# Small buffers placed between the stationary operands of a float32r matmul kernel

## The chip, the cores and the metric

The kernel runs on one core of a Trainium2 chip. The metric is the device time of one execution in microseconds (us). TensorE has two clock levels, 1.2 and 2.4 GHz; the granted clock in the profile is given as a share of the upper one.

## The reference, cut to what matters

Two layers work on an activation of 256 rows by 1024 columns in float32. Each layer is a SwiGLU feed-forward block, a mixer of three attention branches, and a second feed-forward block; a last norm ends it.

```python
for l in range(DEPTH):                                   # 2
    x = x + 0.5 * _swiglu(_rmsnorm(x, ffn1_norm[l]), ffn1_w_gate[l], ffn1_w_up[l], ffn1_w_down[l])
    h = _rmsnorm(x, mix_norm[l])
    ... = jnp.split(h @ w_in[l], cuts, axis=-1)
    y_a = _dsa_attention(...) @ w_branch_a[l]
    y_b = _moba_attention(...) @ w_branch_b[l]
    y_c = _nsa_attention(...) @ w_branch_c[l]
    g = jax.nn.sigmoid(m_g.reshape(B, T, N_BRANCH, D))
    x = x + (g[:, :, 0] * y_a + g[:, :, 1] * y_b + g[:, :, 2] * y_c) @ w_out[l]
    x = x + 0.5 * _swiglu(_rmsnorm(x, ffn2_norm[l]), ffn2_w_gate[l], ffn2_w_up[l], ffn2_w_down[l])
return _rmsnorm(x, final_norm)
```

## The kernel before

Every large product is done with a float32r trick: both operands are split into a high and a low part, and three matmuls replace one (`three`, lines 1371 to 1373): high activation by high weight, high activation by low weight, low activation by high weight. The same three kinds stand in `by_pieces` (line 1421), which serves the first two slabs and the one after them at the start of the kernel.

The weights of the model are the moving operand: a slab of 2048 float32 per partition is loaded by DMA into `raw`, ScalarE writes the high part `whi` (line 1114) and VectorE the low part `wlo` (line 536). Each of the three has three slots of 8192 bytes per partition. A matmul streams 512 columns of a slab (2048 bytes per partition), in the last projection slabs (`M_LAST`) 220 columns, so that there column block kk of a slab begins at kk times 880 bytes.

The activations are the stationary operand, 128 columns of float32 (512 bytes per partition) for each matmul: `ht_hi` and `ht_lo` (the turned, normed x, 8 blocks of 256 columns), `at_hi` and `at_lo` (the gated product of a feed-forward step, or the heads of a branch), and `bt_hi` and `bt_lo` (the same for the step before the last one and for other heads). Each of these 128 columns is loaded into TensorE by an LDWEIGHTS of its own, since no two matmuls in a row have the same stationary operand.

The tensors in SBUF (`sb(...)`) lie one behind another in each partition in the order in which they are declared. Ahead of `ht_hi` stand `raw`, `whi`, `wlo` and `x`, with 24576, 24576, 24576 and 8192 bytes; `ht_hi` and `ht_lo` have 8192 bytes each, `at_*` and `bt_*` 2048 each. All of these are multiples of 512, so every slab's start, every 512-column block and every stationary operand has the same place modulo 512.

The small tensors of the change belong to the attention stage. `cgt` holds the gates of branch C (written at line 1292 by ScalarE, lines 898 and 900 by VectorE), `top8` the eight largest scores of a selection round, `nmax` the negated row maxima (line 751) that the exponentials on ScalarE (line 1247) take as bias, and `den` the row sums, read by the reciprocal at line 785.

The queues: SyncE issues the weight DMAs three slabs ahead; ScalarE and VectorE convert the slabs and do the work of the stage between the conversions; TensorE goes through the slabs in order, with transposes (lines 1390, 1546, 1613, 1672) and the small float32 matmuls of the attention (1585, 1632, 1641) between them. The order is written out by hand and the waits are on semaphores. The change touches neither.

Of the kernel before, what the change touches and what calls it, by code (L numbers as in the profile page):

```python
# [33 lines left out]
P = 128  # L34
SEQ, D, DFF, DEPTH = 256, 1024, 2816, 2
NT = SEQ // P
# [96 lines left out]
def build(nc, x_in, ffn1_w_gate, ffn1_w_up, ffn1_w_down, w_in, cmp_w1_k, cmp_w2_k, cmp_w1_v, cmp_w2_v,  # L133
# [3 lines left out]
    with ctx:  # L137
        def sb(name, shape, dt=F32):
            return ctx.enter_context(nc.sbuf_tensor(name, shape, dt))
# [6 lines left out]
        whi = sb("whi", [P, 3, SLAB], F32R)  # L146
        wlo = sb("wlo", [P, 3, SLAB], F32R)
        x = sb("x", [P, NT, D])
        ht_hi = sb("ht_hi", [P, KD, SEQ], F32R)
        ht_lo = sb("ht_lo", [P, KD, SEQ], F32R)  # L150
        at_hi = sb("at_hi", [P, 2, SEQ], F32R)
        at_lo = sb("at_lo", [P, 2, SEQ], F32R)
        bt_hi = sb("bt_hi", [P, 2, SEQ], F32R)
        bt_lo = sb("bt_lo", [P, 2, SEQ], F32R)
        scr = sb("scr", [P, 4 * SEQ])
# [47 lines left out]
        rstd = sb("rstd", [P, NT])  # L203
        hrstd = sb("hrstd", [P, NT])
        work = sb("work", [P, 384])
        top8 = sb("top8", [P, NT, 8])

        sel_b = sb("sel_b", [P, 384])
        future_b = sb("future_b", [P, 384])
        nmax = sb("nmax", [P, 2, 16])  # L210
        den = sb("den", [P, 2, 16])
        rden = sb("rden", [P, 2, 16])
        cgt = sb("cgt", [P, NT, 24])
        cgt3 = cgt[:, :, :].rearrange("p t (h b) -> p t h b", b=3)
        hid = sb("hid", [P, 64])
        hid2 = sb("hid2", [P, 64])
# [1699 lines left out]
```

## Time and profile before

| | us |
|---|---|
| median of 2 runs | 1163.97 (1163.6 to 1164.35) |
| the profiled execution | 1163.91 |
| its span, first to last instruction | 1162.2 |
| TensorE busy | 1153.9 |
| VectorE busy | 951.5 |
| ScalarE busy | 581.7 |
| GpSimd busy | 31.9 |

The profile is one execution. PE is TensorE's matmuls, PEld its weight loads, which run beside the matmuls. A matmul's record reaches from its start to the end of its drain, so the records of a dense stretch overlap: the distance from one start to the next is what a matmul costs there, not the length of its record. The chain of work that ended last takes that into account. "x4" is a count, "128x512" are partitions by elements.

### The profile page before, as it was taken

How to read it: one execution, taken by the hardware profiler on the slowest of the kernel's cores; microseconds unless marked ns; L12 is line 12 of the kernel's file. 1: busy time of each engine (PE TensorE's matmuls, PEld its weight loads, DVE VectorE, ACT ScalarE, POOL GpSimd, SP SyncE). 2: the span in 40 equal slices, each digit the busy share in tenths (PEclk: the TensorE clock that was granted, in tenths of full speed). 3: DMA queues.
4: the chain of work that ended last, by engine and by line, in shares of the span. 5: the costliest groups of instructions: out<-in, count | busy, mean ns of one | idle time of the engine just before them, and what ended most of it. 6: DMA issues, size and time to landing. Idle time of an engine off the chain costs nothing.

```text
span 1162.2 us, 16328 instructions
## 1 busy us (share of the span) xinstructions
PE 1153.9 (99%) x5573; PEld 945.9 (81%) x5573; DVE 951.5 (82%) x1788; ACT 581.7 (50%) x757; POOL 31.9 (3%) x67
## 2 busy tenths in 40 slices
PE   9999999999999999999999999999999999999997
PEld 7888888887778888888888888888877788888886
DVE  6877788899977687778887887878999696888777
ACT  6444345447764464344454444454578635434433
POOL 2000000001000000000000000000010000000000
PEclk9999999999999999999999999999999999999999
DMA  8566554765425555655556556556653335655561
GB/s 285 190 214 216 181 188 163 234 203 163 137 80 182 181 157 204 217 191 185 195 177 202 180 173 215 182 189 191 198 180 110 141 135 184 219 181 169 202 234 38
DMA packets 148996, 211.04 MB, mean 182 GB/s; under 512 B 8160, under 2 KB 109136, under 8 KB 148944
## 3 DMA queue, kind: packets, MB, share of 16 engines
q1 hardware_dynamic: 148256, 209.64, 54.5%
q10 hardware_dynamic: 688, 0.71, 0.2%
q8 instruction: 31, 0.51, 0.2%
q14 instruction: 21, 0.17, 0.0%
HBM read 209.28 MB, written 1.05 MB: 181 GB/s over the span
## 4 chain that ended last, share of the span: by engine, by line
PE 99%; DVE 0%; issue 0%; ACT 0%; POOLq 0%; POOL 0%; DVEq 0%
PE ps L1371 30%; PE ps L1373 30%; PE ps L1372 30%; PE ps L1585 2%; PE ps L1421 1%; PE ps L1641 1%; PE ps L1613 1%; PE ps L1390 1%; PE ps L1546 1%; PE ps L1558 0%; PE ps L1765 0%; PE ps L1672 0%; PE ps L1632 0%; DVE x L1000 0%; PE ps L1573 0%
## 5 line engine op out<-in xcount | busy, mean ns | idle before, releaser
L1114 ACT ACTIVATE whi<-raw 128x2048 fp32r<-128x2048 f32 (+1 forms) x195 | 365.9, 1879 | 253.3 <-PE ps L1373 252.2
L536 DVE TENSOR_TENSOR wlo<-raw,whi 128x2048 fp32r<-128x2048 f32 (+1 forms) x195 | 433.9, 2244 | 65.6 <-ACT whi L1114 45.7
L1371 PE MATMUL ps<-whi,ht_hi 128*128 128x512 f32 (+1 forms) x1192 | 465.6, 391 | 0.2
L1373 PE MATMUL ps<-whi,ht_lo 128*128 128x512 f32 (+1 forms) x1192 | 460.8, 387 | 0.0
L1372 PE MATMUL ps<-wlo,ht_hi 128*128 128x512 f32 (+1 forms) x1192 | 460.3, 386 | 0.0
L1373 PEld LDWEIGHTS ps<-whi,ht_lo 128*128 128x128 f32 x1192 | 223.9, 188 | 45.9
L1371 PEld LDWEIGHTS ps<-whi,ht_hi 128*128 128x128 f32 x1192 | 224.0, 188 | 45.0 <-issue 1.4
L1372 PEld LDWEIGHTS ps<-wlo,ht_hi 128*128 128x128 f32 x1192 | 224.1, 188 | 43.9
L598 DVE STREAM_TRANSPOSE scr<-scr 32x128 f32<-32x128 f32 x688 | 208.3, 303 | 10.3
L1371 PE MATMUL ps<-whi,at_hi 128*128 128x512 f32 x304 | 118.5, 390 | 0.0
L1372 PE MATMUL ps<-wlo,at_hi 128*128 128x512 f32 x304 | 118.3, 389 | 0.0
L1373 PE MATMUL ps<-whi,at_lo 128*128 128x512 f32 x304 | 118.3, 389 | 0.0
L1154 ACT ACTIVATE scr<-ps,rstd 128x256 f32<-128x256 f32 x88 | 36.9, 471 | 130.7 <-PE ps L1373 130.2
L588 DVE SCALAR_TENSOR_TENSOR scr<-ps,rstd,scr 128x256 f32<-128x256 f32 x88 | 38.5, 479 | 56.0 <-ACT scr L1154 56.0
L1371 PEld LDWEIGHTS ps<-whi,at_hi 128*128 128x128 f32 x304 | 57.1, 188 | 12.5 <-issue 0.8
L1373 PEld LDWEIGHTS ps<-whi,at_lo 128*128 128x128 f32 x304 | 57.1, 188 | 11.9
L1372 PEld LDWEIGHTS ps<-wlo,at_hi 128*128 128x128 f32 x304 | 57.1, 188 | 11.9
L1247 ACT ACTIVATE prob<-prob,nmax 128x128 f32<-128x128 f32 (+1 forms) x96 | 42.4, 446 | 6.7 <-DVE nmax L751 6.7
L1142 ACT ACTIVATE ht_hi<-ps,cols 128x256 fp32r<-128x256 f32 x47 | 19.2, 472 | 30.4 <-PE ps L1390 30.4
L1213 ACT ACTIVATE proj<-ps,rstd 128x512 f32<-128x512 f32 (+1 forms) x24 | 14.2, 645 | 35.6 <-PE ps L1373 35.6
L1260 ACT ACTIVATE p_t<-ps 128x512 f32<-128x512 f32 x36 | 20.1, 592 | 19.6 <-PE ps L1613 14.3
L560 DVE SCALAR_TENSOR_TENSOR ht_lo<-ps,cols,ht_hi 128x256 fp32r<-128x256 f32 x48 | 20.6, 477 | 10.9 <-ACT ht_hi L1142 10.8
(176 smaller groups left out, 757.3 us busy)
## 6 DMA issues: line engine op xcount, KB each, us to landing
raw<-in_ffn_w_down_dram SPq DMA_DIRECT2D x88, 512.0 KB, 4.9
raw<-in_w_in_dram SPq DMA_DIRECT2D x88, 512.0 KB, 4.5
raw<-in_ffn_w_gate_dram SPq DMA_DIRECT2D x85, 512.0 KB, 4.0
raw<-in_ffn_w_up_dram SPq DMA_DIRECT2D x85, 512.0 KB, 5.0
raw<-in_w_out_dram SPq DMA_DIRECT2D x16, 512.0 KB, 4.4
raw<-in_w_branch_c_dram SPq DMA_DIRECT2D x8, 512.0 KB, 4.4
raw<-in_w_branch_b_dram SPq DMA_DIRECT2D x4, 512.0 KB, 3.9
raw<-in_w_branch_a_dram SPq DMA_DIRECT2D x4, 512.0 KB, 4.0
```

Source lines behind the costliest of these rows:

```text
L536: nc.vector.tensor_tensor(wlo[:, n, 0:w], raw[:, n, 0:w], whi[:, n, 0:w].bitcast(F32), ALU.subtract).then_inc(lo_done, 1)
L560: nc.vector.scalar_tensor_tensor(ht_lo[:, k, :], src, gain(l, n, k), ht_hi[:, k, :].bitcast(F32), ALU.mult, ALU.subtract).then_inc(htl, 1)
L588: nc.vector.scalar_tensor_tensor(act[:, t, :], ps[:, bank, FSTEP:2 * FSTEP], rstd[:, t:t + 1], sg[:, t, :], ALU.mult, ALU.mult).then_inc(a ...
L598: ins = nc.vector.transpose(dst[q:q + 32, :, :, a:a + 32], src[a:a + 32, :, :, q:q + 32])
L1114: nc.scalar.activation(whi[:, n, 0:w], raw[:, n, 0:w], ACT.Copy).then_inc(hi_done, 1)
L1154: nc.scalar.activation(sg[:, t, :], ps[:, t + step_bank(f, i), 0:FSTEP], ACT.Silu, scale=rstd[:, t:t + 1]).then_inc(silu_done, 1)
L1247: ins = nc.scalar.activation(pv, pv, ACT.Exp, scale=-1.0, bias=nmax[:, b, 4 * t + h:4 * t + h + 1], accum_out=den[:, b, 4 * t + h:4 * t + ...
L1260: nc.scalar.activation(p_t[:, f, :], ps[:, pt_bank(e, f), :], ACT.Copy).then_inc(pt_a, 1)
L1371: nc.tensor.matmul(o, xh, wh, start=start, stop=False)
L1372: nc.tensor.matmul(o, xh, wl, start=False, stop=False)
L1373: return nc.tensor.matmul(o, xl, wh, start=False, stop=stop)
L1585: ins = nc.tensor.matmul(score_head(t, h), q_t[row, qb + h // 2, t * P:(t + 1) * P], k_t[row, kb + kstep * (h // 2), 0:nk], start=opens, s ...
```

## The change

Four small tensors move in the list of declarations: `cgt` (192 bytes per partition) goes between `x` and `ht_hi`; `top8` (64) and `nmax` (128) go between `ht_lo` and `at_hi`; `den` (128) goes between `at_lo` and `bt_hi`. Against the moving operands, modulo 512, `ht_hi` and `ht_lo` then begin 192 bytes on, `at_hi` and `at_lo` 384 bytes on, and `bt_hi` and `bt_lo` at the same place again, as does everything from `scr` on up to where `top8` stood. The tensors declared behind that place move down by up to 512 bytes. No instruction is added, removed or moved.

```diff
@@ -146,10 +146,14 @@
         whi = sb("whi", [P, 3, SLAB], F32R)
         wlo = sb("wlo", [P, 3, SLAB], F32R)
         x = sb("x", [P, NT, D])
+        cgt = sb("cgt", [P, NT, 24])
         ht_hi = sb("ht_hi", [P, KD, SEQ], F32R)
         ht_lo = sb("ht_lo", [P, KD, SEQ], F32R)
+        top8 = sb("top8", [P, NT, 8])
+        nmax = sb("nmax", [P, 2, 16])
         at_hi = sb("at_hi", [P, 2, SEQ], F32R)
         at_lo = sb("at_lo", [P, 2, SEQ], F32R)
+        den = sb("den", [P, 2, 16])
         bt_hi = sb("bt_hi", [P, 2, SEQ], F32R)
         bt_lo = sb("bt_lo", [P, 2, SEQ], F32R)
         scr = sb("scr", [P, 4 * SEQ])
@@ -203,14 +207,10 @@
         rstd = sb("rstd", [P, NT])
         hrstd = sb("hrstd", [P, NT])
         work = sb("work", [P, 384])
-        top8 = sb("top8", [P, NT, 8])
 
         sel_b = sb("sel_b", [P, 384])
         future_b = sb("future_b", [P, 384])
-        nmax = sb("nmax", [P, 2, 16])
-        den = sb("den", [P, 2, 16])
         rden = sb("rden", [P, 2, 16])
-        cgt = sb("cgt", [P, NT, 24])
         cgt3 = cgt[:, :, :].rearrange("p t (h b) -> p t h b", b=3)
```

## Rows read from the trace of the kernel before

**Rows 1.** The page's chain that ended last: shares of the span, then lines.
```profile
PE 99%; DVE 0%; issue 0%; ACT 0%; POOLq 0%; POOL 0%; DVEq 0%
PE ps L1371 30%; PE ps L1373 30%; PE ps L1372 30%; PE ps L1585 2%; PE ps L1421 1%; PE ps L1641 1%; PE ps L1613 1%; PE ps L1390 1%; PE ps L1546 1%; PE ps L1558 0%; PE ps L1765 0%; PE ps L1672 0%; PE ps L1632 0%; DVE x L1000 0%; PE ps L1573 0%
```
**Rows 2.** Windows by stage: us, busy (xinstructions) per engine, granted clock, DMA share, GB/s.
```profile
600.00:700.00 100.00, 100.00 (x443) 82.81 (x442) 82.88 (x139) 44.42 (x38) 0.00 (x0) 1.00 0.56 188
...
800.00:900.00 100.00, 99.90 (x636) 81.53 (x635) 92.23 (x251) 65.26 (x137) 7.08 (x8) 1.00 0.54 166
```
**Rows 3.** Groups by form, PE, whole span: xcount | busy us, mean ns | idle us.
```profile
L1371 PE MATMUL ps<-whi,ht_hi 128*128 128x512 f32 x1160 | 456.8, 394 | 0.2
L1373 PE MATMUL ps<-whi,ht_lo 128*128 128x512 f32 x1160 | 452.0, 390 | 0.0
L1371 PE MATMUL ps<-whi,at_hi 128*128 128x512 f32 x304 | 118.5, 390 | 0.0
L1371 PE MATMUL ps<-whi,bt_hi 128*128 128x512 f32 x48 | 18.8, 393 | 0.0
L1371 PE MATMUL ps<-whi,ht_hi 128*128 128x220 f32 x32 | 8.8, 275 | 0.0
L1421 PE MATMUL ps<-whi,ht_hi 128*128 128x512 f32 x24 | 8.4, 432 | 0.0
L1632 PE MATMUL ps<-w_k,scr 128*128 128x256 f32 x16 | 4.1, 378 | 0.0
```
**Rows 4.** Timeline of PE, dense stretch: start us, us, instruction.
```profile
624.62 0.39 PE L1371 MATMUL ps<-whi,at_hi 128*128 128x512 f32 x1
...
625.98 0.39 PE L1371 MATMUL ps<-whi,at_hi 128*128 128x512 f32 x1
```
**Rows 5.** The chain in order of time: start us, us, line.
```profile
303.83 0.87 PE ps L1613 x8
...
307.44 0.86 PE ps L1632 x4
```
**Rows 6.** Timeline of PEld around a matmul with no weight load beside it.
```profile
336.81 0.19 PEld L1373 LDWEIGHTS ps<-whi,ht_lo 128*128 128x128 f32 x1
337.35 0.14 PEld L1641 LDWEIGHTS ps<-p_t,proj 128*64 128x64 f32 x2 [0.35 <-issue]
```
**Rows 7.** Groups by form, PE, 337.2 to 337.3 us: that one matmul.
```profile
L1373 PE MATMUL ps<-whi,ht_lo 128*128 128x512 f32 x1 | 0.4, 388 | 0.0
```
**Rows 8.** Groups by form, PE, 336.9 to 337.0 us: its neighbours before.
```profile
L1371 PE MATMUL ps<-whi,ht_hi 128*128 128x512 f32 x1 | 0.4, 389 | 0.0
L1372 PE MATMUL ps<-wlo,ht_hi 128*128 128x512 f32 x1 | 0.4, 389 | 0.0
```
**Rows 9.** Groups by form, PE, 244.86 to 244.90 us: the first narrow matmul.
```profile
L1371 PE MATMUL ps<-whi,ht_hi 128*128 128x220 f32 x1 | 0.3, 262 | 0.0
```
**Rows 10.** Timeline of PE, narrow matmuls: first one counted, and nine starts later.
```profile
245.06 0.27 PE L1373 MATMUL ps<-whi,ht_lo 128*128 128x220 f32 x1
...
246.07 0.27 PE L1373 MATMUL ps<-whi,ht_lo 128*128 128x220 f32 x1
```
**Rows 11.** Groups by form, PEld, 244.93 to 250.2 us: all narrow slabs.
```profile
L1373 PEld LDWEIGHTS ps<-whi,ht_lo 128*128 128x128 f32 x16 | 3.1, 192 | 0.0
L1372 PEld LDWEIGHTS ps<-wlo,ht_hi 128*128 128x128 f32 x16 | 3.1, 192 | 0.0
L1371 PEld LDWEIGHTS ps<-whi,ht_hi 128*128 128x128 f32 x15 | 2.9, 192 | 0.0
```
**Rows 12.** The page's groups, PEld: weight loads beside 512-column streams mostly.
```profile
L1373 PEld LDWEIGHTS ps<-whi,ht_lo 128*128 128x128 f32 x1192 | 223.9, 188 | 45.9
L1373 PEld LDWEIGHTS ps<-whi,at_lo 128*128 128x128 f32 x304 | 57.1, 188 | 11.9
```
**Rows 13.** Who waited for whom: us, times, longest us.
```profile
ACT whi L1114 <- PE ps L1373: 252.2, 93, 3.6
PEld ps L1613 <- DVE prob L804: 0.8, 2, 0.4
```
**Rows 14.** Instructions on nmax, den and cgt: ns min/median/max, us, forms.
```profile
L751 DVE DVE_READ_ACCUMULATOR2_ANT nmax<- x96: 81/83/85, 284.8 to 916.9; 128x1 f32 x96
L785 DVE RECIPROCAL rden<-den x24: 170/177/179, 289.1 to 919.4; 128x4 f32<-128x4 f32 x24
L804 DVE TENSOR_SCALAR prob<-prob,rden,cgt x32: 395/408/749, 299.5 to 904.0; 128x256 f32<-128x256 f32 x32
```

## The prediction

> **What bounds the kernel now.** I read the chain of work that ended last first: TensorE is 99% of it, and the three lines of the three-matmul product alone are 90% [rows 1]. The windows by stage say the same of each part: in a feed-forward stretch TensorE is busy for 100.00 of 100 us, VectorE for 82.88 and ScalarE for 44.42; in the attention stage TensorE 99.90, VectorE 92.23 [rows 2]. The granted clock is 1.00, the upper of the two levels, 2.4 GHz. The list of waits shows ScalarE waiting 252.2 us for TensorE to free a slab, and TensorE's own weight loads waiting 0.8 us for VectorE's scaled probabilities [rows 13]. So the time is a count of matmuls times the distance between two starts, and nothing that VectorE or ScalarE does a little faster or slower is seen.
>
> The count: 1160 + 304 + 48 + 24 groups of three 512-column float32r matmuls, 4608 in all [rows 3]. The distance: seven starts from 624.62 to 625.98 us, six steps, 1.36 / 6 = 0.2267 us [rows 4]. The product is 1044.6 us, 90% of the span, which agrees with the chain. Only this distance can move the time: 1% of it is 10 us.
>
> 512 columns at 2.4 GHz are 213.3 ns, so 13.3 ns of each step are something else. The profile has a yardstick: four plain float32 matmuls of 256 columns, each with its own 128-column weight load, follow each other in 0.86 / 4 = 215 ns [rows 5], and their records last 378 ns where the float32r ones last 389 [rows 3, 8]. So 226.7 - 215 = 11.7 ns are peculiar to the float32r stream. The change can be worth something only if these 11.7 ns, or a part, depend on where the stationary operand lies, or if a new cost appears.
>
> **The change part by part.** *Instructions.* None is added, removed or moved; no wait, no DMA and no queue changes. The moving operands and x don't move. What moves is the address of the stationary operands: 3 x (1160 + 304 + 24) = 4464 wide matmuls now have it 192 bytes (ht) or 384 bytes (at) on; 144 (bt) keep their place modulo 512 and are a control [rows 3].
>
> *The small tensors.* They are used in two short stages: 96 reads of the row maximum at 83 ns, 24 reciprocals at 177 ns, 32 scalings at 408 ns, besides a few more [rows 14]. I take 0. Were each VectorE instruction of these rows 10% slower, that is 0.1 x (96 x 0.083 + 24 x 0.177 + 32 x 0.408) = 2.5 us of VectorE work in all; the cover is VectorE's idle 7.8 us in each 100 of that stage and the slabs converted ahead [rows 2]; without the cover 2.5 us is the price.
>
> *The writes.* ScalarE and VectorE write ht, at and bt at the new addresses. Both have tens of us to spare in each 100 us of a feed-forward stage [rows 2]: 0.
>
> *The weight load itself.* It runs beside the preceding matmul. At its own pace it allows one matmul each 0.87 / 8 = 109 ns (eight 128-column transposes, each with a load of 128 columns) [rows 5]. Beside a wide matmul it has 226.7 ns. A slower load is therefore hidden until it costs 118 ns more, twice its length: 0 for 4464 loads. Only the 96 narrow matmuls of 220 columns are paced by it: were each load 4 ns slower, 0.4 us.
>
> *The stream beside the load.* This is the one term that counts. Both are reads of the same partitions. Today both begin at the same place modulo 512; the stream covers 2048 bytes in 226.7 ns (9.0 bytes per ns) and the load 512 bytes in at most 109 ns (4.7). The stream draws ahead at 4.3 bytes per ns and would come upon the load's place modulo 512 again only after 512 / 4.3 = 119 ns, when the load is over. With the operand 192 bytes on the stream passes it after 45 ns, with 384 after 89 ns, both within the load. If two reads at one place modulo 512 hinder each other, the before is the case with a meeting at the start only, and the after has one in the middle. Does the trace show any hindrance?
>
> First, today's: at 337.03 us a float32r matmul runs with no load beside it; the load before it starts at 336.81, and the next at 337.35 after 0.35 us of idle time [rows 6]. Its record is 388 ns [rows 7]; its neighbours with loads beside them have 389 each [rows 8]. So the load takes 1 ns from the stream and the 11.7 ns are there without it. Against the mean of the whole group of line 1373, 390 ns [rows 3], it is 2 ns. The ends of these records are modelled, which is why I don't call this proof. A second sign is that the excess goes with the columns: the first narrow matmul, not yet held by its weights, has 262 ns [rows 9]; (388 - 262) / 292 columns = 0.432 ns per column where 2.4 GHz gives 0.417. That is a slower stream, not a fixed loss to a load.
>
> Second, another place modulo 512: in the narrow slabs the column blocks begin at 0, 880 and 1760 bytes, that is 0, 368 and 224 modulo 512, so the stationary operand is 0, 144 and 288 bytes on. The 47 loads there all average 192 ns in their three groups [rows 11]; a dependence on place would have to show in them unless it were the same for all three. Beside wide matmuls the load has 188 [rows 12]. The distance is (246.07 - 245.06) / 9 = 112.2 ns [rows 10], against the 109 of the transposes. What this doesn't exclude: these streams have 275 ns against 262, so 13 ns of their record is waiting for weights [rows 3, 9], and a loss of the stream below that would be hidden.
>
> So the value I take for the term is 0 per matmul, the nearest rows in kind being 388 and 389. Below: the meeting of today is worth up to 2 ns, 4464 x 2 = 8.9 us gained. Above: a new meeting costs as much as a narrow stream and a load lose to each other, 112.2 - 108.7 = 3.5 ns, 15.6 us. The farthest bound is that stream and load are served in turn, 109 ns each, 487 us; nothing leans to it.
>
> The Trainium skill, page "TensorE: Matmul & The Clock Gate", section "Part 2: What happens when you issue a matmul", says that stream and weight load have independent read ports, and section "Back-to-back issue gap" gives N / 2.4 + 2.5 ns, 215.8 ns for 512 columns. By the first the change is worth 0, and rows 7 and 8 agree to 1 ns; the second does not agree with the 226.7 ns of rows 4, and were placement the reason for the difference the sum would be near 1115 us.
>
> **Sum.** 1163.9 (the profiled execution, 1162.2 of span and 1.7 around it) + 0 + 0 + 0 = 1163.9 us, the same as the median within 0.1.
>
> **The rivals.**
> *A gain from the end of today's meeting, small:* up to 8.9 us, 1155.0 to 1161 us. For it: 389 against 388. Against it: 1 ns is one tick of the record.
> *A gain that takes the whole excess:* the 11.7 ns of the float32r stream come from both operands at one place modulo 512. 4464 x 11.7 = 52 us: 1112 us; half of it 1138. For it: the excess exists, and every wide matmul has the same placement, so the trace has no wide one to compare. Against it: the lone matmul has it too.
> *A loss: the stream passes the load.* Place: each matmul on ht and at. At 3.5 ns, 1179.5 us; it decides (over 2%) from 23.3 / 4464 = 5.2 ns per matmul, and at 8 ns it gives 1199.6 us. For it: the geometry above, and that rows 10 and 11 can't see a stream loss under 13 ns. Against it: loads at three places with one duration, and no record in a wide stretch that differs between ht, at and bt.
> *The change does nothing to the placement* (padding elsewhere evens it out): 1163.9 us, the same forecast.
>
> **How the numbers follow.** No effect, with or without placement changed: 0.66. Small gain 0.08, large gain 0.06. Loss up to 1179.5: 0.08; from there to 2%: 0.02; beyond: 0.10. The likeliest case's own range is 1161 to 1167 us. The range 1155 to 1180 us takes in the bounds of the term and holds 0.82. About 2% is what a measurement of this kernel can tell from no change: faster 0.06, within 0.84, slower 0.10.
>
> **What would show it.** Right: the steps of a dense stretch stay at 0.2267 us for ht, at and bt alike, records at 389 ns, loads at 188. A loss or gain by placement shows as a step that differs between at or ht and bt in the same profile, in proportion over all stages. A loss through the small tensors would show in the attention windows alone, with waits of weight loads for VectorE above 0.8 us. The forecast falls if the step of ht or at moves by 1 ns or more: then reads of the two operands do meet, and the 1 ns of the lone matmul misled me.

## The result, and the profile after

The changed kernel takes 1176.06 us (1175.56 to 1176.56) against 1163.97: a ratio of 1.0104 with a 95% interval of 1.006 to 1.0147. It is slower by 1%, clear of the noise, though under the 2% that the prediction counts as a change. The forecast was 1163.9, no change; the value lies in the range only because a rival's price was in it.

The page of the changed kernel, its span and the chain that ended last (to be read against [rows 1]):

```profile
span 1174.7 us, 16328 instructions
...
PE 98%; DMA 1%; SPq 0%; issue 0%; DVE 0%; ACT 0%; POOLq 0%; POOL 0%; DVEq 0%
```

Windows by stage of the changed kernel, the columns of [rows 2]:

```profile
600.00:700.00 100.00, 100.00 (x436) 81.59 (x435) 82.42 (x148) 42.78 (x39) 0.00 (x0) 1.00 0.59 197
...
800.00:900.00 100.00, 99.90 (x617) 81.87 (x617) 91.27 (x230) 61.60 (x118) 5.80 (x6) 1.00 0.54 167
```

TensorE is busy throughout and its clock is granted in full, as before. (The 1% of DMA is the arrival of x at the start, for which TensorE's weight load waited 0.9 us. It isn't the loss: e11 below has the same line on its page and loses nothing, and 200 matmuls in, the changed kernel is only 0.15 us behind.) What fell is the number of matmuls in the same 100 us of a feed-forward stretch: 436 in place of 443, 1.6%. The loss is in TensorE's pace and is spread over all stages. Groups by form of the changed kernel, PE, whole span, to be read against [rows 3]:

```profile
L1371 PE MATMUL ps<-whi,ht_hi 128*128 128x512 f32 x1160 | 457.4, 394 | 0.2
L1373 PE MATMUL ps<-whi,ht_lo 128*128 128x512 f32 x1160 | 456.7, 394 | 0.0
...
L1371 PE MATMUL ps<-whi,at_hi 128*128 128x512 f32 x304 | 120.3, 396 | 0.0
...
L1371 PE MATMUL ps<-whi,bt_hi 128*128 128x512 f32 x48 | 18.9, 394 | 0.0
L1373 PE MATMUL ps<-whi,bt_lo 128*128 128x512 f32 x48 | 18.7, 390 | 0.0
```

The records of line 1373 on ht grew from 390 to 394 ns, of line 1371 on at from 390 to 396; bt, the control, has 394 and 390, against 393 and 389 of before; its own first steps, right behind those on at, are slower too. The same ten matmuls of a dense stretch, 40.4 to 42.3 us, groups by form, first the kernel before, then the changed one:

```profile
L1373 PE MATMUL ps<-whi,ht_lo 128*128 128x512 f32 x4 | 1.6, 389 | 0.0
L1371 PE MATMUL ps<-whi,ht_hi 128*128 128x512 f32 x3 | 1.2, 389 | 0.0
L1372 PE MATMUL ps<-wlo,ht_hi 128*128 128x512 f32 x3 | 1.2, 389 | 0.0
```

```profile
L1373 PE MATMUL ps<-whi,ht_lo 128*128 128x512 f32 x4 | 1.6, 394 | 0.0
L1372 PE MATMUL ps<-wlo,ht_hi 128*128 128x512 f32 x3 | 1.2, 392 | 0.0
L1371 PE MATMUL ps<-whi,ht_hi 128*128 128x512 f32 x3 | 1.2, 388 | 0.0
```

Where there was one value there are now three. Timeline of PE in the changed kernel, the first and last start of 28 steps on ht and of 12 steps on at:

```profile
40.11 0.39 PE L1373 MATMUL ps<-whi,ht_lo 128*128 128x512 f32 x1
...
46.52 0.39 PE L1371 MATMUL ps<-whi,ht_hi 128*128 128x512 f32 x1
...
47.21 0.39 PE L1371 MATMUL ps<-whi,at_hi 128*128 128x512 f32 x1
...
50.01 0.39 PE L1371 MATMUL ps<-whi,at_hi 128*128 128x512 f32 x1
```

6.41 / 28 = 228.9 ns on ht and 2.80 / 12 = 233.3 on at, against the 226.7 of [rows 4]. In whole ns the steps on ht go round in 226, 229, 232 and those on at in 229, 237; on bt they settle at 226.7. With the settled means of the whole trace, 2.22 ns over the kernel before on ht and 6.13 on at, the sum is 3552 x 2.22 + 912 x 6.13 = 13.5 us; the span grew by 12.5. It falls a little short since in the first steps after a restart both kernels are slow. Both traces hold the same 5573 matmuls in the same order; compared start by start, the distances on ht grew by 7.1 us in all, those on at by 5.6, those on bt by 0.2, and all others together shrank by 0.3.

### The profile page after: what moved, and what is told of

Same layout as the page of the kernel before. It is cut to its first block, busy times and chain, and to the rows that moved or that the text cites. A ratio compares the mean times of both kernels' runs of the same rounds, so it can differ in the third digit from the quotient of the medians.

```text
span 1174.7 us, 16328 instructions
## 1 busy us (share of the span) xinstructions
PE 1165.8 (99%) x5573; PEld 945.6 (80%) x5573; DVE 951.3 (81%) x1788; ACT 582.0 (50%) x757; POOL 31.8 (3%) x67
## 4 chain that ended last, share of the span: by engine, by line
PE 98%; DMA 1%; SPq 0%; issue 0%; DVE 0%; ACT 0%; POOLq 0%; POOL 0%; DVEq 0%
PE ps L1373 30%; PE ps L1371 30%; PE ps L1372 30%; PE ps L1585 2%; PE ps L1641 1%; PE ps L1613 1%; PE ps L1421 1%; PE ps L1390 1%; PE ps L1546 1%; DMA x<-in_x_dram 1%; PE ps L1558 0%; PE ps L1672 0%; PE ps L1632 0%; SPq L497 0%; DVE x L1000 0%
## 5 line engine op out<-in xcount | busy, mean ns | idle before, releaser
L1373 PE MATMUL ps<-whi,ht_lo 128*128 128x512 f32 (+1 forms) x1192 | 465.5, 391 | 0.0
```

What stands on the lines that cost most here:

```text
L1373: return nc.tensor.matmul(o, xl, wh, start=False, stop=stop)
```

## The experiments

"Place" is from here on how many bytes, modulo 512, the stationary operand begins behind the moving one. A "settled step" is the mean distance of two starts from the 13th matmul of a stretch on, worked out from the starts in the trace; in lone runs of 16 matmuls from the 9th on. Most steps go round in a cycle that this cuts at some point, so that a settled step can be off by up to 1 ns, on at in e12 by 1.4. e9, e10 and e13 are one execution each, and only the steps of their added runs are read.

**Is it the small tensors or the place?** e1 leaves cgt, top8, nmax and den where they were:

```diff
+        pad_ht = sb("pad_ht", [P, 48])
         ht_hi = sb("ht_hi", [P, KD, SEQ], F32R)
         ht_lo = sb("ht_lo", [P, KD, SEQ], F32R)
+        pad_at = sb("pad_at", [P, 48])
         at_hi = sb("at_hi", [P, 2, SEQ], F32R)
         at_lo = sb("at_lo", [P, 2, SEQ], F32R)
+        pad_bt = sb("pad_bt", [P, 32])
         bt_hi = sb("bt_hi", [P, 2, SEQ], F32R)
```

> The kernel before with three unused tensors of 192, 192 and 128 bytes per partition ahead of ht_hi, at_hi and bt_hi; cgt, top8, nmax and den stay where they were. Theory P (the time comes from where the stationary operands lie against the moving ones, modulo 512): the same as the changed kernel, 1176 us (1174 to 1178), steps of a dense stretch 226/229/232 ns on ht, 229/237 ns on at, 227 ns on bt. Rival S (the moved small tensors cost it): 1164 us and 226.7 ns everywhere.

Measured: 1176.27 us against 1163.39, ratio 1.0110 (1.0094 to 1.0127), settled steps 228.9, 232.9 and 226.7 ns. The small tensors cost nothing; the place costs it all.

**The operand's own place or the distance?** e2 moves the moving operands as well, so that ht is aligned and the distances are the changed kernel's:

```diff
+        pad_front = sb("pad_front", [P, 80])
         raw = sb("raw", [P, 3, SLAB])
         ...
+        cgt = sb("cgt", [P, NT, 24])
         x = sb("x", [P, NT, D])
-        cgt = sb("cgt", [P, NT, 24])
         ht_hi = sb("ht_hi", [P, KD, SEQ], F32R)
         ...
         bt_lo = sb("bt_lo", [P, 2, SEQ], F32R)
+        pad_scr = sb("pad_scr", [P, 48])
```

(against the changed kernel)

> raw, whi and wlo begin 320 bytes on, x at 0, ht at 0, at at 192, bt at 320, scr at 0, modulo 512: the distances of the stationary operands from the moving ones are those of the changed kernel (192, 384, 0), but ht is aligned and at is not. Theory D (only the distance counts): 1176 us, and the steps of the changed kernel: ht 229.0 ns on average, at 233.2, bt 226.7. Rival A (an operand's own place counts, as a stationary operand that lies across a 512-byte boundary): ht costs nothing, at about 229, bt more than 226.7; some 1166 to 1170 us.

Measured: 1176.46 us, ratio 1.0111 (1.0094 to 1.0128); settled steps 228.9, 232.9, 226.7. Groups by form of e2, PE:

```profile
L1375 PE MATMUL ps<-whi,ht_lo 128*128 128x512 f32 x1160 | 456.9, 394 | 0.0
...
L1373 PE MATMUL ps<-whi,at_hi 128*128 128x512 f32 x304 | 120.3, 396 | 0.0
```

The aligned ht has the 394 ns it had at 192. At these places only the distance counts.

**Do the two parts add?** e3 pads 192 bytes ahead of ht_hi and 320 ahead of at_hi; e4 pads 384 ahead of at_hi and 128 ahead of bt_hi.

> The kernel before with 192 unused bytes ahead of ht_hi and 320 ahead of at_hi: ht is 192 bytes on, at and bt are where they were modulo 512. Theory P: 3552 matmuls at 229.0 in place of 226.7 ns, 1164.0 + 8 = 1172 us; at steps stay at 226.7 ns. Rival (the cost arises where the stream changes between operands at different places): less than 1168 us.

> The kernel before with 384 unused bytes ahead of at_hi and 128 ahead of bt_hi: at is 384 bytes on, ht and bt are where they were modulo 512. Theory P: 912 matmuls at 233.2 in place of 226.7 ns, 1164.0 + 6 = 1170 us; ht steps stay at 226.7 ns. Rival (the cost arises where the stream changes between operands at different places): 1166 us or less, with the cost in the first steps after a change.

Measured: 1170.10 us (ratio 1.0056, 1.0039 to 1.0073) and 1169.83 (1.0055, 1.0038 to 1.0072): 6.7 and 6.4 us over the 1163.39 of their runs of before, 13.1 together against e1's 12.9. Groups by form, first e3, then e4:

```profile
L1373 PE MATMUL ps<-whi,ht_hi 128*128 128x512 f32 x1160 | 459.9, 397 | 0.2
...
L1373 PE MATMUL ps<-whi,at_hi 128*128 128x512 f32 x304 | 118.5, 390 | 0.0
```

```profile
L1373 PE MATMUL ps<-whi,ht_hi 128*128 128x512 f32 x1160 | 456.7, 394 | 0.2
...
L1373 PE MATMUL ps<-whi,at_hi 128*128 128x512 f32 x304 | 120.5, 396 | 0.0
```

Each moved operand pays for itself, the other keeps the figure of before (394 and 390). The rival of both expectations falls: both times lie above its 1168 and 1166 us, and the settled steps, 228.9 on ht in e3 and 232.9 on at in e4, carry the cost. The 912 matmuls at 384 cost as much as the 3552 at 192.

**How does it depend on the place?** e5, e6 and e7 have the pads 64, 64, 128, 256; 320, 128, 32, 32; and 32, 64, 64, 352 bytes ahead of ht_hi, at_hi, bt_hi and scr.

> Unused bytes ahead of ht_hi (64), at_hi (64), bt_hi (128) and scr (256): ht 64, at 128, bt 256 bytes on, modulo 512. Theory M (the stream passes the load's place while the load runs, cost from any distance between 0 and 512): ht about 1 to 3 ns over 226.7, at and bt 2 to 7, the time 1168 to 1180 us. Rival R (what counts is the distance modulo 256 or 128): bt at 256 shows 226.7 ns, with 128 at as well, and ht alone costs.

> ht 320, at 448, bt 480 bytes on, modulo 512. Theory M: ht between the 229.0 of 192 and the 233 of 384, say 231 ns, at near the end of the load and so 227 to 235, bt at 480 as at 0; time 1172 to 1184 us. Rival R (modulo 128): ht at 320 is as 64, at at 448 as 64, bt at 480 as 96.

> ht 32, at 96, bt 160 bytes on, modulo 512. Theory M: ht nearly as at 0, 226.7 to 228 ns, at 227 to 230, bt 228 to 230; time 1164 to 1172 us. Rival G (there is a place that is better than the same one, since 215 ns is the pace of the plain float32 matmuls): a step under 226.7 ns for one of the three, the time below 1163 us if it is ht.

Measured: 1189.46 us (ratio 1.0222), 1188.51 (1.0214), 1192.14 (1.0246). The first and the last are more than 2% slower beyond the noise; of the second the interval is 1.0197 to 1.0231. Groups by form of e7, PE, where [rows 3] have 390 for both:

```profile
L1377 PE MATMUL ps<-whi,ht_lo 128*128 128x512 f32 x1160 | 458.7, 395 | 0.0
...
L1375 PE MATMUL ps<-whi,at_hi 128*128 128x512 f32 x304 | 120.8, 397 | 0.0
```

Settled steps in ns, with those of the runs above:

| place | 0 | 32 | 64 | 96 | 128 | 160 | 192 | 256 | 320 | 384 | 448 | 480 |
|---|---|---|---|---|---|---|---|---|---|---|---|---|
| step | 226.7 | 233.4 | 233.4 | 234.0 | 231.8 | 233.6 | 228.9 | 226.7 | 233.4 | 232.8 to 233.0 | 230.4 | 233.3 |

Taken by whole cycles, 128 and, in e4, 384 have 232.4 ns, 96 has 234.3, and 32, 64, 160, 320 and 480 all have 233.3. Theory M falls: 32 bytes, which the stream passes first, cost three times what 192 do, and 480 is not near 0. Rival R holds in its coarse form: 256 is as 0, 320 as 64, and e11 (below) confirms it in time; its finer form, modulo 128, falls. Rival G falls as well: no place gave less than 226.7. 384 shows in e4 the same round of steps as 128 in e5 (230, 233, 241, 232, 231, 232, 228); in the changed kernel and in e1 most stretches at 384 go round in 229, 237 instead, so one place can settle in more than one way. 448 does what 192 does in some stretches and in others keeps the 233 of the ht stretch before it. The changed kernel's 192 was the mildest place of all but 0.

**One operand of the three.** e8 pads 192 bytes ahead of ht_lo and 320 ahead of at_hi.

> Unused bytes ahead of ht_lo (192) and at_hi (320): of all stationary operands ht_lo alone is 192 bytes on. Its loads run beside one stream in three, that of ht_hi by wlo. Theory L (the loss arises where the load beside the stream lies elsewhere): only that step or the one after it is longer, a third to two thirds of what ht_hi and ht_lo cost together, 1166 to 1169 us. Rival (the distances of two loads in a row count): as much as both together or more, 1170 us or over.

Measured: 1177.11 us, ratio 1.0117 (1.01 to 1.0133), 13.5 us, twice e3's 6.7 though a third of the loads moved. The step on ht is 231.2 ns, mostly in a round of twelve (236, 228, 233, 241, 238, 231, 231, 224, 232, 227, 226, 226), with the steps of all three lines in it. Theory L falls: the cost is not in the stream beside the moved load. One of the three kinds of step has 228, 238, 224 and 226 ns within a single round: what a step costs goes with the steps before it.

**A map with nothing else running.** e9 adds behind the last matmul of the kernel before:

```diff
+            flat = ht_hi[:, :, :].rearrange("p k c -> p (k c)")
+            for place in range(0, 256, 4):
+                for _ in range(16):
+                    nc.tensor.matmul(ps[:, 0, :], flat[:, place // 4:place // 4 + P], whi[:, 0, 0:512], start=True, stop=True)
```

> The kernel before, and behind its last matmul 64 runs of 16 more, each of 512 columns of whi by 128 columns of ht_hi, which begin 0, 4, 8 ... 252 bytes on from the stream's place; VectorE and ScalarE are idle but for the end of the kernel. Their results are not used. Theory B (stream and weight load meet in a structure that repeats every 256 bytes): the settled step is 226.7 ns at 0, near 233 at 32, 64, 96, 128 and 160, 229 at 192, 233 at 224, as in the kernel proper, and in between it changes at a unit of 16, 32 or 64 bytes. Rival O (the other engines' accesses take part): other steps than in the kernel proper. Open: whether a place not divisible by 32 gives less than 226.7 ns; a step near 215 ns there would be worth up to 50 us.

Measured, settled steps in ns, every place divisible by 32 and the others that stand out:

| place | 0 | 32 | 64 | 96 | 128 | 160 | 192 | 224 | 100 | 120 | 132 | 144 | 156 | 204 | 228 | 252 |
|---|---|---|---|---|---|---|---|---|---|---|---|---|---|---|---|---|
| step | 226.6 | 233.6 | 233.0 | 234.3 | 233.9 | 233.0 | 229.3 | 233.1 | 230.0 | 226.6 | 226.7 | 226.6 | 226.7 | 226.6 | 226.6 | 226.7 |

At the places of 32 the lone runs agree with the kernel proper within 0.6 ns but at 128 (2.1), so rival O falls: VectorE and ScalarE have no part in it. The other 48 places lie between 228.3 and 236.3. Of theory B the unit of 16, 32 or 64 bytes falls: places 4 bytes apart differ (140 has 233.4, 144 has 226.6). No place of the 64 is below 226.6: the kernel before already had the best of these, and none of them gives back any of the 11.7 ns.

**Is it the load beside the stream?** e10 adds runs with narrower stationary operands, fewer moving columns, and alternating places:

```diff
+            for place in (0, 64, 128, 192):
+                for width in (128, 96, 64, 32):
+                    for _ in range(16):
+                        nc.tensor.matmul(ps[0:width, 0, :], flat[:, place // 4:place // 4 + width], whi[:, 0, 0:512], start=True, stop=True)
```

> The kernel before, and behind its last matmul runs of 16 more whose stationary operand has 128, 96, 64 or 32 columns, at 0, 64, 128 and 192 bytes on; then runs with 512, 384 and 256 moving columns at 0, 64, 192; then runs whose stationary operand alternates between two places. Their results are not used. Theory C (the stream loses time while a weight load reads beside it): the excess over 215 ns falls with the width, at place 64 from 18 ns at 128 columns to some 5 at 32, at place 0 from 11.7 to 3. Rival F (the excess belongs to the float32r stream itself): 226.7 ns at place 0 for every width, the part by place alone falls. Theory C for fewer moving columns: the excess in ns is the same, 12 and 18; rival F: it goes with the columns. Alternating places: 0 with 256 and 64 with 320 as one place alone.

Groups by form of e10, PE, all four places together:

```profile
L1782 PE MATMUL ps<-whi,ht_hi 128*32 128x512 f32 x64 | 15.4, 394 | 0.0
L1782 PE MATMUL ps<-whi,ht_hi 128*96 128x512 f32 x64 | 15.4, 393 | 0.0
L1782 PE MATMUL ps<-whi,ht_hi 128*128 128x512 f32 x64 | 15.4, 392 | 0.0
L1782 PE MATMUL ps<-whi,ht_hi 128*64 128x512 f32 x64 | 15.4, 392 | 0.0
```

A load of a quarter of the width costs the stream as much. Settled steps at place 0 for 128, 96, 64 and 32 columns: 226.6, 229.9, 229.6, 231.7 ns; at 64: 233.3, 227.9, 232.3, 230.4. Theory C falls. The place matters at every width, but not by time in which load and stream read side by side. Fewer moving columns at place 0: 384 give 173.3 ns and 256 give 120.0, in both 13.3 more than the columns take at 2.4 GHz, so rival F's share of the columns falls as well; at place 64, 256 columns give 113.3. Alternating 0 and 256: 226.7, as one place alone; alternating 0 and 128: 233.3.

**The same four tensors at a harmless place.** e11:

```diff
+        cgt = sb("cgt", [P, NT, 24])
+        top8 = sb("top8", [P, NT, 8])
         ht_hi = sb("ht_hi", [P, KD, SEQ], F32R)
         ht_lo = sb("ht_lo", [P, KD, SEQ], F32R)
+        nmax = sb("nmax", [P, 2, 16])
+        den = sb("den", [P, 2, 16])
         at_hi = sb("at_hi", [P, 2, SEQ], F32R)
```

> The same four small tensors go between the operands, but in pairs that make 256 bytes: cgt and top8 ahead of ht_hi, nmax and den ahead of at_hi; ht lies 256 bytes on, at and bt at 0, modulo 512. Theory Q (the place repeats every 256 bytes and only it counts): 1164 us and 226.7 ns everywhere. Rival: anything of the small tensors or of the half of a 512-byte block counts: over 1166 us.

Measured: 1163.73 us against 1163.67, ratio 1.0001 (0.9991 to 1.001), settled steps 226.7 on all three. Groups by form:

```profile
L1371 PE MATMUL ps<-whi,ht_hi 128*128 128x512 f32 x1160 | 456.7, 394 | 0.2
...
L1371 PE MATMUL ps<-whi,at_hi 128*128 128x512 f32 x304 | 118.5, 390 | 0.0
```

**Do the fine places carry over?** e12 takes ht_hi, ht_lo as slices of one tensor that begin 144 bytes on, and at_hi, at_lo likewise at 204:

```diff
+        pad_ht = sb("pad_ht", [P, 32])
+        ht = sb("ht", [P, 2 * KD * SEQ + 8], F32R)
+        ht_hi = ht[:, 4:4 + KD * SEQ].rearrange("p (k c) -> p k c", k=KD)
+        ht_lo = ht[:, 4 + KD * SEQ:4 + 2 * KD * SEQ].rearrange("p (k c) -> p k c", k=KD)
```

> ht lies 144 bytes on, at 204, bt 256, places at which the lone runs behind the kernel settled at 226.6 ns though their neighbours 4 bytes off had 230 to 234. Theory Q: the kernel proper settles there too, at most some steps after each change of operand are longer: 1164 to 1168 us. Rival H (in the kernel proper high and low parts and wlo differ, so that the fine places don't carry over): 1175 to 1192 us, as at 128, 160 and 192.

Measured: 1190.97 us, ratio 1.0230 (1.0213 to 1.0247); settled steps 233.2 on ht and, in a round of seven (229, 226, 231, 254, 238, 233, 236), 233.9 on at, 235.3 by whole rounds. The time is rival H's, but its reason falls, since ht at 144 does run at 226.7 ns in six stretches. Those are the six that follow directly on a stretch on bt, which lies at 256 and has found that pace; there ht keeps it from its first step to its last. Timeline of PE of e12, the first and the last start of one of them:

```profile
187.65 0.39 PE L1376 MATMUL ps<-whi,ht 128*128 128x512 f32 x1
...
191.50 0.39 PE L1378 MATMUL ps<-whi,ht 128*128 128x512 f32 x1
```

3.85 / 17 = 226.5 ns, with all three kinds of matmul in it. Behind transposes or a stretch on at, the same operands at the same place settle at about 233.3. So at 144 two paces are possible, and what ran before decides which. For 204 no such stretch exists in the kernel.

**A period or a constant?** e13 varies the moving columns, then shifts the moving operand:

```diff
+            for place in (0, 64, 192):
+                for n in (512, 508, 504, 500, 496, 492, 488, 480, 464, 448, 320):
+                    for _ in range(16):
+                        nc.tensor.matmul(ps[:, 0, 0:n], flat[:, place // 4:place // 4 + P], whi[:, 0, 0:n], start=True, stop=True)
```

> The kernel before, and behind its last matmul runs of 16 with 512, 508, 504, 500, 496, 492, 488, 480, 464, 448 and 320 moving columns at places 0, 64 and 192, then 512 columns with the moving operand begun 0 to 256 bytes on. Results not used. Theory T (something with a period of 16 clocks of 2.4 GHz, 6.67 ns, joins each matmul: a settled constant step is a whole number of such periods): 512 to 500 columns all keep 226.7 ns at place 0 or drop by 6.67 ns at once, and 496, 480, 464, 448 and 320 give 220.0, 213.3, 206.7, 200.0 and 146.7. Rival K (a constant is added to the columns): each 4 columns less shorten the step by 1.67 ns. For the moving operand's shift: at 64, 128 and 192 bytes the steps are those of the stationary operand's place at 192, 128 and 64.

Settled steps in ns; "c" where the steps are one constant value (226 and 227 in turn count as one, 226.7):

| columns | 512 | 508 | 504 | 500 | 496 | 492 | 488 | 480 | 464 | 448 | 320 |
|---|---|---|---|---|---|---|---|---|---|---|---|
| place 0 | 226.7 c | 227.7 | 226.7 c | 223.7 | 223.3 | 222.7 | 225.7 | 216.6 | 208.7 | 202.6 | 146.7 c |
| place 64 | 233.0 | 229.3 | 229.0 | 220.0 c | 219.7 | 220.0 c | 220.3 | 217.1 | 213.3 c | 202.0 | 147.0 |
| place 192 | 229.3 | 229.6 | 228.3 | 229.1 | 226.4 | 226.7 c | 220.6 | 217.9 | 209.9 | 200.3 | 146.7 |

Groups by form of e13, PE, the three places together; 504 columns have the record of 508:

```profile
L1782 PE MATMUL ps<-whi,ht_hi 128*128 128x504 f32 x48 | 11.5, 391 | 0.0
L1782 PE MATMUL ps<-whi,ht_hi 128*128 128x508 f32 x48 | 11.5, 391 | 0.0
```

Rival K falls: at place 0 eight columns less change nothing, at place 192 twenty columns less take off 2.7 ns, at place 64 twelve less take off 13. Theory T is right in part: all constant steps in this table, and the 113.3, 120.0 and 173.3 of e10, are whole multiples of 6.67 ns, 16 clocks of 2.4 GHz. But most combinations don't settle at one, as the theory had said that they would; in e9 place 100 stands constant at 230.0 ns, which is 34.5 periods, and in e10 256 columns at place 192 at 117.7. What holds is a wider form, worked out from the starts: in 120 of the 140 lone runs of e9, e10 and e13 the steps repeat in rounds of one to eight, and the length of the whole round is a multiple of 6.67 ns to within 0.4 ns in all but these two. Two steps of the one (460.0 ns) and three of the other (353.3) are multiples as well. The rounds of the kernels fit: 226 + 229 + 232 ns is 103 periods, 229 + 237 is 70, the seven of e4 are 244, the twelve of e8 are 416. At multiples of 64 the moving operand's shift does what the distance says: 64 bytes give 226/229/232 (as place 192), 128 give 229/237 (as 128), 192 give 231/236 (as 64), and 256 settles at 226.7. At finer shifts it need not: 16 bytes give 232.0 ns, where the same distance in e9 (place 240) gave 228.3.

## Why the prediction was wrong

**What bounds the kernel** was right, and so was the accounting: the time is the number of wide matmuls times the step, and 1% of the step is 10 us. The small tensors, the writes and the weight load's own length at 0: right (e1, e11; the loads stay at 188 ns).

**The step that failed** is "the value I take for the term is 0 per matmul". It measured 2.2 ns on ht and 6.1 on at, 3.0 on average over the 4464 matmuls (13.5 us). The prediction's own sign of failing, a step on ht or at that moves by 1 ns or more, is what came. Two readings led to the 0.

The first reading was the lone matmul: 388 ns with no load beside it, 389 with one [rows 7, 8], hence no hindrance, hence no effect of the place. The middle inference was fair, and e10 bears it out: a load a quarter as wide costs as much. The last was not: that load and stream don't share time doesn't mean that the place doesn't count. The changed kernel's lone matmuls show what the record really tells. At 284.25 and at 291.65 us one runs with no load beside it; the weight loads around the first (timeline of PEld):

```profile
284.03 0.19 PEld L1373 LDWEIGHTS ps<-whi,ht_lo 128*128 128x128 f32 x1
284.58 0.30 PEld L1585 LDWEIGHTS ps<-k_t,q_t 64*128 64x128 f32 x4 [0.36 <-issue]
```

and the two records (groups by form, 284.45 to 284.50 and 291.85 to 291.90 us):

```profile
L1373 PE MATMUL ps<-whi,ht_lo 128*128 128x512 f32 x1 | 0.4, 397 | 0.0
```

```profile
L1373 PE MATMUL ps<-whi,ht_lo 128*128 128x512 f32 x1 | 0.4, 388 | 0.0
```

Same line, same kind of operands, no load: 9 ns apart. It is not the modelled end alone, since the next start comes 326 ns after the first and 318 after the second. In the round of three the first stands where the 232 ns step is, the second where the 226 is. So the loss doesn't need a load beside the stream; it goes with what ran before, and the lone matmul of before with its 388 came out of a row of 226.7.

The second sign that went with it, 0.432 ns per column from a narrow matmul's record, hence "a slower stream, not a fixed loss", was wrong too: at place 0 the steps of 512, 384 and 320 columns settle at 226.7, 173.3 and 146.7 ns, each 13.3 over its columns at 2.4 GHz (e10, e13).

The second reading was the narrow slabs: loads of 192 ns at three places [rows 11]. It looked at the load where the stream was in question, and in a stretch that the load paces. The changed kernel has the same there (groups by form, PEld, 247.9 to 253.2 us):

```profile
L1373 PEld LDWEIGHTS ps<-whi,ht_lo 128*128 128x128 f32 x16 | 3.1, 192 | 0.0
L1372 PEld LDWEIGHTS ps<-wlo,ht_hi 128*128 128x128 f32 x15 | 2.9, 192 | 0.0
```

192 ns again, and 111.7 ns from start to start over 44 steps in both kernels, at a place that costs 2.2 ns in the wide stretches. The prediction said itself that a stream's loss under 13 ns would be hidden there; then the rows could not speak for 0, and I let them.

**What the trace of before did show.** A step that is 226 or 227 ns for hundreds of matmuls looks less like an average of small losses than like a state that repeats itself, and the trace has what happens outside of it. Timeline of PE of the kernel before, behind a restart in the attention stage:

```profile
269.38 0.39 PE L1372 MATMUL ps<-wlo,ht_hi 128*128 128x512 f32 x1
...
270.99 0.39 PE L1373 MATMUL ps<-whi,ht_lo 128*128 128x512 f32 x1
...
273.03 0.39 PE L1373 MATMUL ps<-whi,ht_lo 128*128 128x512 f32 x1
```

Seven steps of 1.61 / 7 = 230.0 ns, then nine of 2.04 / 9 = 226.7. In ns the seven are 230, 231, 236, 228, 233, 231 and 226: losses of up to 9 ns with the same operands at the same place, gone once the pace is found. Of the 17 lone float32r matmuls of line 1373 in the kernel before, 15 have 388 ns and two, in short stretches behind a restart, 397; in the changed kernel 15 have 396 or 397 and two 388. I read one of the 15.

**The rivals.** The loss was priced at up to 3.5 ns per matmul and 1179.5 us; the average was 3.0. Its size was near by luck: the price came from the narrow stretch, which has nothing to do with it, and the mechanism, the stream passing the load, is refuted by the places 32 and 256 and by the narrow loads. Of the two gains the map shows neither: nothing lies below 226.6 ns. That the change does nothing to the placement is refuted by e1.

**The rule weighed.** The Trainium skill, "TensorE: Matmul & The Clock Gate", section "Part 2: What happens when you issue a matmul", gives stream and weight load ports of their own. e10 agrees as far as it goes, since the width of the load doesn't count; that placement is therefore free, as I read it, the runs contradict by 1 to 2.5% of the kernel's time. The 215.8 ns of the section "Back-to-back issue gap", which it gives for a matmul by itself, was reached by none of the 512-column float32r runs here, whose means are 226.6 ns and more.

**What stays open.** Why a distance of 0 or 256 bytes lets the pace settle at 226.7 ns and the others not. The runs show that a matmul's loss depends on what ran before it, that whole rounds of steps are multiples of 6.67 ns, and that at multiples of 64 bytes only the distance of the two operands counts. They do not show which unit keeps the 6.67 ns; a stream with no weight loads at all wasn't tried, as each matmul issues its own.

## What to carry to other kernels

Where TensorE is the bound and each matmul of 512 float32r columns has a new stationary operand of 128, let both operands begin at the same place modulo 256 bytes: small tensors declared between them have to come in multiples of 256 bytes (e11: 1.0001), or behind them all. In this kernel every other multiple of 32 that was tried cost 2 to 7 ns per matmul, up to 2.5% of the time, with no wait anywhere in the profile to show it. And when a step that should vary is constant, look at what it does after a restart before you take a lone sample for the rule.

## What the runs showed of the hardware that I had not expected

- The pace of dense float32r matmuls depends on the distance between the starts of the two operands: 226.7 ns at 0 and 256 bytes, 228.9 at 192, 231.8 to 234.0 at 32 to 160 (512 columns, the granted clock at 2.4 GHz).
- At place 144 the same stretch of matmuls runs at 226.7 ns when it follows on matmuls that have that pace, and at about 233.3 otherwise (e12).
- The pace does not depend in one direction on the width of the load: 226.6 ns at 128 columns, 231.7 at 32 (place 0).
- Settled paces that are constant: 113.3, 120.0, 146.7, 173.3, 213.3, 220.0, 226.7 and 233.3 ns, all multiples of 6.67 ns; 230.0 at place 100 and 117.7 (256 columns at 192) are not. The others go round in cycles, such as 2 (229, 237), 3 (226, 229, 232), 7 or 12 steps, whose sums are multiples of 6.67 ns, and fewer columns need not be faster: 504 take as long as 512 at place 0.
- Moving one operand of three (ht_lo) cost 13.5 us, moving ht_hi with it 6.7.
